# Output projection of a chunk: by halves of the channels, or by halves of the output columns

## The reference, cut to what matters

```
y_l = jnp.concatenate([m_l, y_hy_l], axis=-1).astype(xl.dtype) @ w_out[l]     # (2048, 1024) @ (1024, 1024)
new_xl = xl + gate_l[:, None] * rms_norm(y_l, post_gain[l])
```

## Time and profile before

| what | us |
|---|---|
| median of 3 runs (1963.19 to 1963.88) | 1963.23 |
| the profiled execution's own time | 1962.42 |
| its span, first to last instruction | 1960.6 |
| PE busy in the span | 1763.2 (90%) |
| DVE busy | 709.6 (36%) |
| ACT busy | 679.4 (35%) |
| POOL busy | 233.5 (12%) |

### The profile page before, as it was taken

How to read it: one execution, slowest core, us unless ns; L and a number is a source line. 1 busy time by engine, 2 the same in 40 slices (tenths; PEclk the granted TensorE clock), 3 DMA queues, 4 the chain that set the end, 5 groups by cost and what they waited for, 6 DMA issues and landing times. The chain is left out here.

```text
span 1960.6 us, 27449 instructions
## 1 busy us (share of the span) xinstructions
PE 1763.2 (90%) x10766; PEld 1545.5 (79%) x10766; DVE 709.6 (36%) x1108; ACT 679.4 (35%) x1377; POOL 233.5 (12%) x249
## 2 busy tenths in 40 slices
PE   7469999999999999999969999989999656699998
PEld 3358899888888899998767888888887546688886
DVE  1952310233333320001033525444453236566663
ACT  1433321333222222111134453534444234455442
POOL 0730000000000000000000000000000000566562
PEclk9569999999999999999989999999999878799999
DMA  7321122212221122111161020020010445666662
GB/s 251 117 71 66 70 73 68 69 70 80 81 70 70 70 71 68 67 67 46 49 279 49 23 87 28 23 87 27 22 65 1 136 144 152 187 191 193 186 194 70
DMA packets 125384, 183.16 MB, mean 93 GB/s; under 512 B 10248, under 2 KB 93630, under 8 KB 117728
## 3 DMA queue, kind: packets, MB, share of 16 engines
q1 hardware_dynamic: 125280, 181.71, 27.9%
HBM read 129.04 MB, written 52.64 MB: 93 GB/s over the span
## 5 line engine op out<-in xcount | busy, mean ns | idle before, releaser
L304 PE MATMUL bank<-h_hi,w_hi 128*128 128x512 f32 (+1 forms) x840 | 324.2, 386 | 7.9 <-DVE w_lo L582 7.9
L305 PE MATMUL bank<-h_lo,w_hi 128*128 128x512 f32 (+1 forms) x840 | 323.6, 385 | 0.0
L306 PE MATMUL bank<-h_hi,w_lo 128*128 128x512 f32 (+1 forms) x840 | 323.6, 385 | 0.0
L304 PE MATMUL bank<-w_hi,h_hi 128*128 128x256 f32 x800 | 226.5, 283 | 0.0
L305 PE MATMUL bank<-w_lo,h_hi 128*128 128x256 f32 x800 | 226.4, 283 | 0.0
L306 PE MATMUL bank<-w_hi,h_lo 128*128 128x256 f32 x800 | 226.4, 283 | 0.0
L304 PEld LDWEIGHTS bank<-h_hi,w_hi 128*128 128x128 f32 x840 | 159.0, 189 | 39.7 <-issue 8.5
L305 PEld LDWEIGHTS bank<-h_lo,w_hi 128*128 128x128 f32 x840 | 159.0, 189 | 31.2 <-issue 0.2
L306 PEld LDWEIGHTS bank<-h_hi,w_lo 128*128 128x128 f32 x840 | 159.0, 189 | 31.2
L593 DVE SCALAR_TENSOR_TENSOR work<-work,coef 128x504 f32<-128x504 f32 (+1 forms) x84 | 61.4, 731 | 288.4 <-ACT work L444 288.4
L582 DVE TENSOR_TENSOR w_lo<-stage,w_hi 128x2048 fp32r<-128x2048 f32 (+1 forms) x19 | 43.7, 2304 | 308.2 <-ACT w_hi L424 305.6
(11 more groups left out here) (190 smaller groups left out, 2944.9 us busy)
## 6 DMA issues: line engine op xcount, KB each, us to landing
stage<-in_w_in SPq DMA_DIRECT2D x18, 1024.0 KB, 5.3
s_qhy<-work SPq DMA_DIRECT2D x64, 256.0 KB, 2.2
kq<-s_k SPq DMA_DIRECT2D x34, 256.0 KB, 5.2
v<-s_v SPq DMA_DIRECT2D x34, 256.0 KB, 5.3
stage<-in_w_mod SPq DMA_DIRECT2D x8, 1024.0 KB, 4.9
stage<-in_x SPq DMA_DIRECT2D x16, 512.0 KB, 3.4
s_ozh<-work SPq DMA_DIRECT2D x64, 128.0 KB, 1.7
xin<-s_qhy SPq DMA_DIRECT2D x8, 1024.0 KB, 4.8
```

What stands on the lines that cost most here:

```text
L304: pe.matmul(out, lhs[0], rhs[0], start=(k == 0), stop=False)
L305: pe.matmul(out, lhs[0], rhs[1], start=False, stop=False)
L306: return pe.matmul(out, lhs[1], rhs[0], start=False, stop=(k == KD - 1))
```

## The change

`out_part(n, ks)` becomes `out_half(n, c)`: the first call does all 8 channel blocks of the first 512 output columns, the second all 8 of the second 512. The first call waits for both `yh_lo` and `ym_lo`. Each call waits only for its own bank to have been read (`z_ready` at 2n-1+c). `acc_ready` is counted after each half, so ACT can square the first bank before the second is summed; the other users of `acc_ready` wait for twice the count. The number and shape of the matmuls stay.

```diff
-            def out_part(n, ks):
-                if ks[0]:
+            def out_half(n, c):
+
+                if c == 0:
                     pe.wait_ge(yh_lo, n + 1)
-                    if n:
-                        pe.wait_ge(z_ready, 2 * n)
-                    else:
-                        pe.wait_ge(gate_step, 3)
-                        pe.wait_ge(wo_low, 2)
-                else:
                     pe.wait_ge(ym_lo, n + 1)
-                for c in range(2):
-                    o, cut = acc[c][:, :], slice(c * TILE, (c + 1) * TILE)
-                    for k in ks:
-                        pe.matmul(o, y_hi[:, k, :], w_hi[:, k, cut], start=(k == HEADS), stop=False)
-                        pe.matmul(o, y_hi[:, k, :], w_lo[:, k, cut], start=False, stop=False)
-                        mm = pe.matmul(o, y_lo[:, k, :], w_hi[:, k, cut], start=False, stop=(k == HEADS - 1))
-                if not ks[0]:
-                    mm.then_inc(acc_ready, 1)
+                if n:
+                    pe.wait_ge(z_ready, 2 * n - 1 + c)
+                elif c == 0:
+                    pe.wait_ge(gate_step, 3)
+                    pe.wait_ge(wo_low, 2)
+                o, cut = acc[c][:, :], slice(c * TILE, (c + 1) * TILE)
+                for k in range(KD):
+                    pe.matmul(o, y_hi[:, k, :], w_hi[:, k, cut], start=(k == 0), stop=False)
+                    pe.matmul(o, y_hi[:, k, :], w_lo[:, k, cut], start=False, stop=False)
+                    mm = pe.matmul(o, y_lo[:, k, :], w_hi[:, k, cut], start=False, stop=(k == KD - 1))
+                mm.then_inc(acc_ready, 1)
...
-                    out_part(n - 2, range(HEADS, KD))
-                    out_part(n - 2, range(HEADS))
+                    out_half(n - 2, 0)
+                    out_half(n - 2, 1)
...
-                act.wait_ge(acc_ready, n + 1)
...
                 for c in range(2):
+                    act.wait_ge(acc_ready, 2 * n + c + 1)
                     act.activation(squared_out[c], acc[c][:, :], ACT.Square, accum_out=sumsq[:, b, c:c + 1]).then_inc(squared, 1)
...
-                    act.wait_ge(acc_ready, n)
+                    act.wait_ge(acc_ready, 2 * n)
```

## The result

| | before | changed |
|---|---|---|
| median us | 1963.21 (1962.42 to 1963.88, 4 runs) | 2034.1 (2032.96 to 2038.06, 4 runs) |
| ratio, 95% interval | | 1.0365 (1.0347 to 1.0383), slower |
| span of the profiled execution | 1960.6 | 2031.2 |

The change costs 3.6%, 70.9 us between the medians and 70.6 us between the two spans. 2027.9 us was forecast, in a range of 2004 to 2040.

The account below looks back on a forecast made before the run. PE was taken to bound the kernel, with a load ring nearly as long. Waits of 44.4 us plus clock falls of 20.3 made 64.7 on top of 1963.2: 2027.9 us, range 2004 to 2040.

Parts of the forecast that it names:

- The bound: Loops with projections: PE busy 224.95 of 229.00 us, idle only for the Hyena half of y_lo; 16.40 us a loop.
- second ring: From residual through SP's store, next loads, POOL, ACT and DVE back to residual: nearly as long as PE's loop.
- The added wait: PE's first column half also waits for ym_lo: 19.26 us a loop, 2.86 more than 16.40, +37.2 over thirteen loops.
- the ring: DVE to PE to DVE: numerators' end, DVE up to ym_lo, 48 projection matmuls, numerators; sum 19.26 us a loop.
- It just fits: After the last projection matmul, ACT's handover, DVE's gate, L1408 and residual take 3.4 us, against 3.7 of numerators.
- The ends: First projection's start +3.6 us, chunk 14's loop +3.0, last chunk +1.2, square and gate at the very end -0.6.
- Early square and gate: ACT's first square and DVE's first gate, 0.6 us each, move beside PE's second half; worth nothing more in the loops.
- The load ring off the path: First square possible 12.4 us after the numerators' end, second bank summed at 15.5: about 3 us of slack for loads.
- The clock: PE's holes of about 3 us drop its clock to 0.50: 13 falls in 15 holes, 1.56 us each, 20.3 us.
- The rule cited for the change: Running one output tile's channel tiles together keeps PE at full clock; by that the sum would be 44.4 us alone.
- clock holds: Rival: PE's clock stays up as PE is full for 16 of 19 us; 2007.6 us, chance 14%.

Follow-up runs that it names:

- e6: Kernel before, with SP's program turned so the next loads go ahead of the store: 1958.05 us, ratio 0.9983.
- e5: Changed kernel plus 12 extra matmuls, result unused, ahead of PE's wait for y: 2006.01 us, ratio 1.0236.
- e1: Kernel before with only PE's wait for ym_lo added ahead of the Hyena blocks: 2038.44 us, ratio 1.0406.
- e2: Changed kernel with DVE's low_mlstm moved to the head of its loop, ahead of heads_out: 1970.01 us, ratio 1.0052.
- e4: Changed kernel with the Hyena blocks first in each column half, ym_lo awaited only ahead of the first half's mLSTM blocks: 1963.60 us, ratio 1.0024.
- e7: Kernel before, channel order kept, with SP's loads ahead of the store and acc_ready counted per column half: 1955.16 us, ratio 0.9964.
- e3: Kernel before, channel order kept, with acc_ready counted per column half so ACT may square the first bank early: 1959.18 us, ratio 0.9987.
- e9: Changed kernel plus 6 extra matmuls, result unused, ahead of PE's wait for y: 2020.27 us, ratio 1.0304.
- e10: Changed kernel plus 3 extra matmuls, result unused, ahead of PE's wait for y: 2025.57 us, ratio 1.0331.

## Why the prediction was right, step by step

The mechanism was right, step for step; one term of the sum, the clock's, was sized low, and one part of it was a guess that happened to fit.

- **The bound** (PE with next to no holes, a second ring through the loads at its heels): right. e6 took the second ring away and left 15.91 us a loop.
- **The added wait, +37.2 for thirteen loops:** 19.22 us for the one loop at the full clock, 19.34 in e5, 19.26 forecast. e1 showed the wait alone to be enough, e2 and e4 that without it hardly anything remains. Each piece of the ring is in the timelines within 0.1 us of its forecast, but for the projection, which the clock makes longer.
- **"It just fits" (gates and `residual` within the numerators):** just not. From the fourth projection on L1376 starts 0.12 us behind the numerators' end, and 0.04 before that: `residual` waited 0.45 us for POOL and held DVE 0.08 us too long. That is about 1 us in all.
- **The ends, +3.6, +3.0, +1.2, -0.6:** measured +4.8, +4.5, +3.3 and -0.6. The second and third contain a fall of the clock each (1.5). Of the first, 1.4 us was there before the projections began (transposes at 1698.73 and at 1697.30 before), which the change doesn't touch. The third has 0.45 us of POOL's delay.
- **Early square and gate, nothing in the loops:** as far as can be told. e7 has the same 15.91 us a loop as e6 without it, but there PE has no hole to give; in e3 at most 1.8 us in thirteen loops. At the last chunk and the end it is worth 2.8 us in the order by channels, where 0.6 was counted for the end.
- **The load ring off the path:** right. ACT still waited 6.09 us ahead of its weights in the loop shown, but its second square then waited 3.31 us for PE, as forecast.
- **The clock, 13 falls of 1.56 us:** the term that was sized low, by over 3 us. There were 14 more falls than before, a single one cost 1.4 to 1.5 us (a loop of 20.63 against 19.22, a projection of 12.67 against 11.13), the two long ones 2.8 each (22.15 against 19.34): 12 x 1.5 + 2 x 2.8 = 23.6 us in place of 20.3, and the profiles of the changed kernel and e5 give 23.2 (24.8 less the last chunk's). The forecast of 2027.9 was 6.2 us short: about 3.3 from the clock, 1.2 from the start of the projections, 1 from the `residual` wait, 0.5 from the last chunk. That nearly every hole brings a fall was taken from two cases; e9 and e10 show that the length of a hole does not settle it, so that 13 came close to 14 is in part luck.
- **The rule cited for the change,** all channel blocks of one output tile in a row to keep the clock up (the Trainium skill, page "TensorE: Matmul & The Clock Gate", section "HAM oscillation — how this bites in real kernels"): not borne out here. The row was as long as before; what made the clock fall is the hole that this very order opened.
- The rival "clock holds" (2007.6, that is +44.4) is what e5 made: 2006.01, +46.7 on its own chip.

## What to carry to other kernels

Before a first matmul is made to need all its inputs, ask which of them comes last and what PE did meanwhile: the half of the work that needed only the early input was the cover for the late one. A shorter path behind the sum (early square) is worth little while another ring, here the loads queued behind a store, decides when it may run; look for who comes last. On PE a hole can cost twice, once as time and once through the clock, here half as much again; how often the clock falls has to be measured, as holes of the same length went either way.

## What the runs showed of the hardware that was not expected

POOL's single-column power instruction (L986) took 1.05 us in 13 of 16 loops of the changed kernel and 0.56 in all 16 of the kernel before. What differs is the start of DVE's L1406, which reads two operands from SBUF. Two loops of the changed kernel, DVE and POOL:

```profile
1715.91 0.71 DVE L1406 TENSOR_TENSOR y_lo<-yh,y_hi 128x512 fp32r<-128x512 f32 x1
1715.89 0.56 POOL L986 TENSOR_TENSOR root_o<-root_o,power_o 128x1 f32<-128x1 f32 x1
...
1757.11 0.68 DVE L1406 TENSOR_TENSOR y_lo<-yh,y_hi 128x512 fp32r<-128x512 f32 x1
1757.15 1.05 POOL L986 TENSOR_TENSOR root_o<-root_o,power_o 128x1 f32<-128x1 f32 x1
```

Where POOL starts 0.02 us ahead of DVE it takes 0.56, where it starts 0.04 us behind it, 1.05. Over the changed kernel, the kernel before, e2, e4 and e7, that is 80 instances, it took 1.05 in all 28 with a start 0.04 to 0.05 us behind L1406's, and 0.56 in all others. The Trainium skill, page "SBUF — State Buffer", section "Who interferes with whom", has a rule for it: a DVE instruction with two SBUF inputs contends with a GpSimd instruction that reads SBUF, over a port pair that the two engines share as an exclusive lock. The traces agree where DVE comes first: POOL's instruction ends 0.49 us later. The other way round they show next to nothing: in the two cases of the changed kernel with POOL 0.02 us ahead, DVE's instruction takes 0.71 us in place of 0.68. In e1, where the two squares follow each other as before, all 16 took 0.56. A likely reason, read from the program and not tested by itself: the early square leaves only the last gate between ACT's sum and L1406, so L1406 and POOL's third step come due at the same moment. It takes both the early square and loads that are not late: 11 of 16 in e7, which has both, against 2 in e3, none in e6 and none in the kernel before.
